# Moving the forget gate's sums one pair of projections back, with their room and their loads in another order

## The chip, the core and the metric

The kernel runs on one core of a Trainium2 chip. The metric is the time of one execution on the device in microseconds (us), the median of several runs; lower is better. TensorE (PE in the rows) multiplies matrices, VectorE (DVE) and ScalarE (ACT) work on elements, GpSimd (POOL) masks, sets constants and issues some DMAs, and the queue of SyncE (SP) issues nearly all loads.

## What is computed

Two layers of a decoder trunk, float32, 528 tokens (16 learned ones and 512 given) of 1024 channels. Each layer is a half-step feed-forward block, a mixer, and another half-step feed-forward block. The change lies in the mixer of the first layer, the attention, whose reference is, cut to what matters:

```python
def attn_mixer(h, w_in, b_f, w_out):
    proj = h @ w_in                      # 24 strips of 128 columns, and 8 columns of forget gates
    qa, ka, va = heads(0), heads(1), heads(2)      # 8 stick-breaking heads of 64
    qb, kb, vb = heads(3), heads(4), heads(5)      # 8 forgetting heads of 64
    log_f = jax.nn.log_sigmoid(f_logit + b_f)
    c = jnp.cumsum(log_f, axis=1)                  # the forget gate's sums, 8 heads x 528 tokens
    ...
    s = jnp.einsum('bhqd,bhkd->bhqk', qb, kb) * scale
    s = s + c[:, :, q0:q1, None] - c[:, :, None, :q1]
    p = jax.nn.softmax(jnp.where(causal, s, -jnp.inf), axis=-1)
    ...
    return jnp.concatenate([o_sb, o_fox], axis=-1) @ w_out
```

The sums `c` are added to the scores of the forgetting heads. They are needed at the first scores of those heads, and no sooner.

## The kernel before

Every product is made at float32 accuracy out of three products of rounded parts: high by high, high by low, low by high. So each weight tile is split, a high part written by ScalarE (`w_hi`) and a low part by VectorE (`w_lo`), and TensorE reads both.

The projections (24 strips) are four plain strips and then ten pairs of strips, `ph.pairs[0]` to `ph.pairs[9]`; pair n holds the strips `p.f` = 4 + 2n and the next. With `QK = 16`, pair 6 (`p.f == QK`) is the first of the pairs that give values; the pairs before it give queries and keys. A pair is computed with seven quarter-size products instead of eight (`qkv_pe`): TensorE's order in pair n is product 1 of n, product 3 of n-1, product 2 of n, product 6 of n, product 4 of n-1, product 7 of n, product 5 of n, each of 12 matmuls. Each has weights of its own. VectorE makes their low parts in a fixed order written out in `attn_dve`: `s23_low` (L2240, for product 6), then drains and sums of weights (L1352, L2213, L1345, L2219, L2224), `s14_low` (L2245, for product 5), for the query and key pairs a low part of the results (L1319), `a_low` of the next pair (L2229, for its products 1 and 2), more drains (L1338, L1359, L1365), and `a22_low` of the next pair (L2234, for its product 4). ScalarE goes through a matching order of its own (`attn_act`).

The forget gate's chain lies between these steps. ScalarE has its logarithm ready long before. At the end of pair 6, VectorE ends the gate (L1436) and sums it over the tokens (L1438, the scan); this counts `fg_step` up to 5. In pair 7 ScalarE writes the high parts of the sums, with both signs (L1195, L1196, `c_high`), and at the end of pair 7 VectorE the low parts (L1441, L1442, `c_low`). GpSimd then stores the four rows of parts to memory (`c_dram`, L3294, `c_stored`).

The gate, its logarithm, the sums and a row of ones (`fg`, `fg_abs`, `fg_sum`, `fg_one`) are the slots 0 to 3 of `fg_room`. That room is shared: the slots are where the first head's queries `sb_qq`, `sb_ql` (slots 0 and 1), its forgetting queries `fx_qq` (slot 2) and its forgetting keys `fx_kk` (slot 3) are loaded later.

`stage_heads` writes out the order of SyncE's queue: the keys of the first head (4 loads), after the wait for `c_low` the queries and the forgetting queries and keys (8 loads), after the wait for `c_stored` two rows twice of the sums (`stage_sums`, 4.1 KB each), then four weight strips of the output projection (`fetch_out`, 512 KB each). The first two strips go as soon as `a22_low` of pair 8 is done, the other two once `a22_low` of pair 9 is. All 14 loads of the first head count one semaphore, `staged[0]`. TensorE waits for all of them at `first_scores`, in pair 9 between its products 4 and 7.

## Time and profile before

| what | us |
|---|---|
| median of 3 runs | 1757.29 (1756.66 to 1757.46) |
| the profiled execution, its time | 1756.96 |
| its span on the core | 1755.2 |
| TensorE busy | 1739.5 |
| VectorE busy | 1401.1 |
| ScalarE busy | 939.0 |
| GpSimd busy | 71.8 |

The span is what the engines' records cover; the time also has what lies around it, 1.76 us here. Busy time is summed from each engine's records, with matmul ends modelled. In a timeline row, a number in brackets is time in which the engine stood idle ahead of the instruction, with what ended it; a matmul's record lasts 0.28 us while the next one starts 0.12 us after it, so the distance between starts tells more of TensorE than the records' lengths.

### The profile page before, as it was taken

To read this page: it belongs to the slowest core of one execution; us is meant where nothing else is said; L and a number is where in the kernel's file an instruction comes from. 1 tells how busy PE (TensorE), PEld (TensorE's weight loads), DVE (VectorE), ACT (ScalarE), POOL (GpSimd) and SP (SyncE) were. 2 spreads that over 40 slices of the span, in tenths; PEclk is the share of its full clock that TensorE was granted. 3 is DMA by queue.
4 is the path that set the end of the run, shared out by engine and by line. 5 is a ranking of instruction groups with operands and counts; after the bars stand their busy time and mean duration, and the time that the engine had idled before them with its cause. 6 is when DMAs were issued, how large, how long until landed. Compare 5 with 4: busy or idle time off the path is not lost.

```text
span 1755.2 us, 34355 instructions
## 1 busy us (share of the span) xinstructions
PE 1739.5 (99%) x13600; PEld 1693.1 (96%) x13600; DVE 1401.1 (80%) x2018; ACT 939.0 (53%) x1554; POOL 71.8 (4%) x193
## 2 busy tenths in 40 slices
PE   8999999999999999999999999999999999999998
PEld 8999999999998899999999999999999988899997
DVE  6856998789988858848998688489987788499875
ACT  6433655555578844625655546246555445266555
POOL 0000000002122202000000000000000000000000
PEclk9999999999999999999999999999999999999999
DMA  5243333236655332333343323333342323343332
GB/s 159 85 121 97 97 108 110 80 103 197 196 157 149 88 109 85 97 97 97 97 119 92 102 87 108 97 96 97 97 113 74 91 77 104 89 114 110 97 95 74
DMA packets 334087, 187.01 MB, mean 107 GB/s; under 512 B 17713, under 2 KB 324593, under 8 KB 333937
## 3 DMA queue, kind: packets, MB, share of 16 engines
q1 hardware_dynamic: 330144, 175.31, 35.6%
q0 software_dynamic: 2960, 8.98, 1.4%
q8 instruction: 106, 1.74, 0.4%
q10 hardware_dynamic: 832, 0.62, 0.1%
q14 instruction: 45, 0.36, 0.1%
HBM read 171.58 MB, written 10.88 MB: 104 GB/s over the span
## 4 chain that ended last, share of the span: by engine, by line
PE 88%; DVE 8%; issue 2%; ACT 1%; DMA 1%; POOL 0%; DVEq 0%; ACTq 0%; SPq 0%; POOLq 0%
PE pair L2820 50%; PE pair L2792 18%; PE pair L2761 8%; PE pair L3156 4%; PE pair L2807 1%; PE pair L968 1%; PE pair L988 1%; PE pair L3032 1%; PE pair L2998 1%; DVE sums_w L2213 1%; DVE w_lo L2245 1%; DVE w_lo L2240 1%; DVE qk_lo L1319 1%; PE pair L903 0%; PE pair L885 0%
## 5 line engine op out<-in xcount | busy, mean ns | idle before, releaser
L2820 PE MATMUL pair<-b_hi,w_hi 128*128 128x264 f32 (+1 forms) x1464 | 415.9, 284 | 0.0
L2820 PE MATMUL pair<-b_lo,w_hi 128*128 128x264 f32 (+1 forms) x1464 | 415.0, 283 | 0.0
L2820 PE MATMUL pair<-b_hi,w_lo 128*128 128x264 f32 (+1 forms) x1464 | 414.6, 283 | 0.0
L2820 PEld LDWEIGHTS pair<-b_hi,w_hi 128*128 128x128 f32 x1464 | 275.7, 188 | 0.9 <-issue 0.5
L2820 PEld LDWEIGHTS pair<-b_hi,w_lo 128*128 128x128 f32 x1464 | 275.7, 188 | 0.0
L2820 PEld LDWEIGHTS pair<-b_lo,w_hi 128*128 128x128 f32 x1464 | 275.6, 188 | 0.0
L1738 ACT ACTIVATE w_hi<-sums_w 128x1024 fp32r<-128x1024 f32 x188 | 198.6, 1057 | 104.7 <-PE pair L2820 60.9
L1738 ACT ACTIVATE w_hi<-raw_all 128x1024 fp32r<-128x1024 f32 (+1 forms) x188 | 158.9, 845 | 141.9 <-PE pair L2820 101.2
L2820 PE MATMUL pair<-blocks_hi,w_hi 128*128 128x264 f32 (+1 forms) x816 | 231.3, 283 | 0.3 <-ACT parts L1925 0.3
L2820 PE MATMUL pair<-blocks_lo,w_hi 128*128 128x264 f32 (+1 forms) x816 | 231.5, 284 | 0.0
L2820 PE MATMUL pair<-blocks_hi,w_lo 128*128 128x264 f32 (+1 forms) x816 | 230.8, 283 | 0.0
L2792 PE MATMUL pair<-b_hi,w_lo 128*128 128x264 f32 (+1 forms) x766 | 173.8, 298 | 0.0
L2792 PE MATMUL pair<-b_hi,w_hi 128*128 128x264 f32 (+1 forms) x766 | 173.5, 298 | 0.0
L2792 PE MATMUL pair<-b_lo,w_hi 128*128 128x264 f32 (+1 forms) x766 | 173.4, 298 | 0.0
L2131 DVE TENSOR_TENSOR w_lo<-raw_all,w_hi 128x1024 fp32r<-128x1024 f32 x117 | 142.6, 1221 | 28.2 <-ACT w_hi L1709 28.2
L1709 ACT ACTIVATE w_hi<-raw_all 128x1024 fp32r<-128x1024 f32 x117 | 121.7, 1050 | 63.3 <-PE pair L2792 58.8
L2820 PEld LDWEIGHTS pair<-blocks_hi,w_hi 128*128 128x128 f32 x816 | 153.8, 188 | 0.7 <-ACT parts L1925 0.5
L2820 PEld LDWEIGHTS pair<-blocks_hi,w_lo 128*128 128x128 f32 x816 | 153.7, 188 | 0.0
L2820 PEld LDWEIGHTS pair<-blocks_lo,w_hi 128*128 128x128 f32 x816 | 153.5, 188 | 0.2
L2240 DVE TENSOR_TENSOR w_lo<-sums_w,w_hi 128x1024 fp32r<-128x1024 f32 x94 | 114.8, 1221 | 24.0 <-ACT w_hi L1738 24.0
L2637 DVE SCALAR_TENSOR_TENSOR h<-pair,h 128x528 f32<-128x528 f32 (+1 forms) x61 | 42.9, 703 | 109.0 <-PE pair L2792 108.4
L2245 DVE TENSOR_TENSOR w_lo<-sums_w,w_hi 128x1024 fp32r<-128x1024 f32 x94 | 114.6, 1219 | 17.8 <-ACT w_hi L1738 17.6
(355 smaller groups left out, 3788.1 us busy)
## 6 DMA issues: line engine op xcount, KB each, us to landing
raw_all<-in_w_ffn_in SPq DMA_DIRECT2D x173, 512.0 KB, 4.0
raw_all<-in_w_ffn_out SPq DMA_DIRECT2D x64, 512.0 KB, 4.4
raw_all<-in_w_ffn_out SPq DMA_DIRECT2D x32, 384.0 KB, 3.7
raw_all<-in_w_attn_in SPq DMA_DIRECT2D x24, 512.0 KB, 4.7
q_all<-qk_dram SPq DMA_DIRECT2D x48, 132.0 KB
qk_dram<-qk_hi POOLq DMA_DIRECT2D x16, 264.0 KB, 4.5
qk_dram<-qk_lo POOLq DMA_DIRECT2D x16, 264.0 KB, 3.0
raw_all<-in_w_attn_out SPq DMA_DIRECT2D x8, 512.0 KB, 4.9
```

What stands on the lines that cost most here:

```text
L968: mm = nc.tensor.matmul(o_main[:, 0, q0 - META:SEQ], head_v[e][:, 0, 3 - s, :], w[:, 0:nq], start=(g == 0), stop=True, skip_group_check=True)
L988: mm = nc.tensor.matmul(own, head_v[e][:, 1, b, :], turned_p[s][:, b, :], start=(g == 0 and b == 0), stop=True, skip_group_check=True)
L1709: nc.scalar.activation(w_hi[j][:, :], raw[j][:, :], ACT.Copy).then_inc(hi_ready, 1)
L1738: return nc.scalar.activation(dst, src, ACT.Copy)
L2131: nc.vector.tensor_tensor(w_lo[j][:, :], raw[j][:, :], w_hi[j][:, :], ALU.subtract).then_inc(lo_ready, 1)
L2240: nc.vector.tensor_tensor(w_lo[1][:, :], S23, w_hi[1][:, :], ALU.subtract).then_inc(s23_lo, 1)
L2245: nc.vector.tensor_tensor(w_lo[2][:, :], s14(p.q), w_hi[2][:, :], ALU.subtract).then_inc(s14_lo, 1)
L2637: nc.vector.scalar_tensor_tensor(hm, pair_of(OUT_BANK[m], ph.last), 0.5, hm, ALU.mult, ALU.add).then_inc(drained, 1)
L2761: mm = nc.tensor.matmul(psum[j][:, bank, c0:c0 + cols], w[j][:, blk], rhs[v][:, k, t0:t0 + cols], start=(k == 0 and w is w_hi and v == 0), ...
L2792: mm = nc.tensor.matmul(bank_of[:, bank, c0:c0 + cols], w[slot][:, blk], rhs[v][:, k, from_:from_ + cols], start=(k == 0 and w is w_hi and ...
L2820: mm = nc.tensor.matmul(dst, w[slot][:, c0 + kk * P:c0 + (kk + 1) * P], rhs(v, kk), start=(fresh and kk == 0 and w is w_hi and v == 0), st ...
L3156: mm = nc.tensor.matmul(psum[j][:, bank, c0:c0 + cols], w[j][:, blk], X[v][:, k, t0:t0 + cols], start=(k == 0 and w is w_hi and v == 0), s ...
```

## The change

The gate's end and the scan move from the end of pair 6 to the end of pair 7 (`p.f == QK + 2`). ScalarE's high parts move from pair 7 to pair 8. VectorE's low parts move from the end of pair 7 into pair 8, behind `s14_low` and ahead of `a_low` of pair 9. Sums and ones change their slots of `fg_room`: the ones now lie where `fx_qq` comes, the sums where `fx_kk` comes. The loads of the queries and of `fx_qq` wait for the scan (`fg_step` at 5), those of `fx_kk` for `c_low`, and the four strips of the output projection come ahead of the loads of the sums. No instruction is added or taken away but for waits.

```diff
--- before.py
+++ after.py
@@ -290,7 +290,7 @@
             turned_p.append(c_room[:, at:at + (i + 2) * P].rearrange("p (b q) -> p b q", q=P).bitcast(F32))
         probs = [qk_room[:, 5 * P:7 * P], b0_rows[:, 1, 7, :], sq, qk_room[:, 0:5 * P]]
 
-        fg, fg_abs, fg_sum, fg_one = (fg_room[0:NH, i, :] for i in range(4))
+        fg, fg_abs, fg_one, fg_sum = (fg_room[0:NH, i, :] for i in range(4))
         fg_both, fg_low = fg_room[:, 0, :], fg_room[LOW_ROW:, 0, :]
         qkv_x = v_rows[:, :, :].rearrange("p (b a) t -> p b (a t)", a=2)
         c_dram = nc.dram_tensor("c_dram", [4, NH, T], F32).ap()
@@ -793,13 +793,17 @@
                 sp.wait_ge(qk_stored[i], stored_before(QK + i))
             sp.wait_ge(aug_ones, 3)
             stage_keys(0, 0)
+            sp.wait_ge(fg_step, 5)
+            stage_queries(0, 0)
+            put(0, fx_qq[0][0:HD, :], part(0, 0, 8))
+            put(0, fx_qq[0][HD:P, :], part(0, 1, 8))
             sp.wait_ge(c_low, 2)
-            stage_queries(0, 0)
-            stage_forgetting(0, 0)
+            put(0, fx_kk[0][0:HD, :], part(0, 0, 12))
+            put(0, fx_kk[0][HD:P, :], part(0, 0, 12))
+            for j in range(4):
+                fetch_out(j)
             sp.wait_ge(c_stored, 16)
             stage_sums(0, 0)
-            for j in range(4):
-                fetch_out(j)
             sp.wait_ge(p5_done, ph.pairs[-1].s + 1)
             stage_queries(0, 1)
             sp.wait_ge(aug_ones, 6)
@@ -1190,7 +1194,7 @@
                 if prev is not None:
                     p1_copy(ph, p, two)
                     s14_high(p, prev)
-                    if prev.f == QK:
+                    if prev.f == QK + 2:
                         act.wait_ge(fg_step, 5)
                         nc.scalar.activation(c_parts[:, 0, :], fg_sum, ACT.Copy).then_inc(c_high, 1)
                         nc.scalar.activation(c_parts[:, 2, :], fg_sum, ACT.Copy, scale=-1.0).then_inc(c_high, 1)
@@ -1417,6 +1421,12 @@
                     s14_low(p)
                     if prev.f < QK:
                         qk_low(prev.f)
+                    if p.f == QK + 4:
+                        dve.wait_ge(c_high, 2)
+                        nc.vector.tensor_tensor(c_parts[:, 1, :], fg_sum, c_parts[:, 0, :],
+                                                ALU.subtract).then_inc(c_low, 1)
+                        nc.vector.tensor_tensor(c_parts[:, 3, :], c_parts[:, 0, :], fg_sum,
+                                                ALU.subtract).then_inc(c_low, 1)
                 if prev is not None and nxt is not None:
                     a_low(nxt)
                 c11_out(p)
@@ -1430,16 +1440,12 @@
                     bottom_scaled(prev)
                 if nxt is not None:
                     a22_low(nxt)
-                if p.f == QK:
+                if p.f == QK + 2:
                     dve.wait_ge(fg_act, 3)
                     dve.wait_ge(fg_step, 3)
                     nc.vector.scalar_tensor_tensor(fg, fg, 0.0, fg_abs, ALU.min, ALU.subtract).then_inc(fg_step, 1)
                     dve.wait_ge(fg_step, 4)
                     nc.vector.tensor_tensor_scan(fg_sum, fg_one, fg, 0.0, ALU.mult, ALU.add).then_inc(fg_step, 1)
-                elif p.f == QK + 2:
-                    dve.wait_ge(c_high, 2)
-                    nc.vector.tensor_tensor(c_parts[:, 1, :], fg_sum, c_parts[:, 0, :], ALU.subtract).then_inc(c_low, 1)
-                    nc.vector.tensor_tensor(c_parts[:, 3, :], c_parts[:, 0, :], fg_sum, ALU.subtract).then_inc(c_low, 1)
 
             def dve_mask(hp, g):
                 s, c = g % 4, STEPS * hp + g
```

On VectorE, around the end of pair 6, before (L1436 and L1438 are the gate's end and the scan, `w_lo<-sums_w` at L2240 is the low part for product 6 of pair 7):

```order
L1365 SCALAR_TENSOR_TENSOR qk_room<-qk_room,qkv_scale,rinv 128x528 [waits drained]
L2234 TENSOR_TENSOR w_lo<-raw_all,w_hi 128x512 [waits hi_ready]
L1436 SCALAR_TENSOR_TENSOR fg_room<-fg_room 8x528 [waits fg_step,fg_act]
L1438 SCALAR_TENSOR_TENSOR fg_room<-fg_room 8x528 [waits fg_step]
L2240 TENSOR_TENSOR w_lo<-sums_w,w_hi 128x1024 [waits s23_hi]
L1319 TENSOR_TENSOR qk_lo<-qk_room,qk_hi 128x528 [waits qk_high_done]
L1352 TENSOR_TENSOR v_rows<-pair,qkv_parts 128x264 [waits qkv_t_lo,u4_out,p7_done]
```

And now (all lines of this part of the program are 4 to 6 higher; L2246 was L2240):

```order
L1369 SCALAR_TENSOR_TENSOR qk_room<-qk_room,qkv_scale,rinv 128x528 [waits drained]
L2240 TENSOR_TENSOR w_lo<-raw_all,w_hi 128x512 [waits hi_ready]
L2246 TENSOR_TENSOR w_lo<-sums_w,w_hi 128x1024 [waits s23_hi]
L1323 TENSOR_TENSOR qk_lo<-qk_room,qk_hi 128x528 [waits qk_high_done]
L1356 TENSOR_TENSOR v_rows<-pair,qkv_parts 128x264 [waits qkv_t_lo,u4_out,p7_done]
```

The two steps of the gate no longer stand ahead of the low part for product 6 of pair 7. On VectorE from the end of pair 7 to `a_low` of pair 9, before:

```order
L1441 TENSOR_TENSOR c_room<-fg_room,c_room 8x528 [waits c_high]
L1442 TENSOR_TENSOR c_room<-c_room,fg_room 8x528
L2240 TENSOR_TENSOR w_lo<-sums_w,w_hi 128x1024 [waits s23_hi]
L1352 TENSOR_TENSOR v_rows<-pair,qkv_parts 128x264 [waits qkv_t_lo,u4_out,p7_done]
L2213 TENSOR_TENSOR sums_w<-raw_all 128x2x512 [waits s23_lo,s14_lo,landed3,landed2]
L1345 SCALAR_TENSOR_TENSOR v_rows<-pair,qkv_scale,rinv 128x264 [waits qkv_t_lo,unit_done]
L2219 TENSOR_TENSOR sums_w<-sums_w,raw_all 128x512 [waits s13_done]
L2224 TENSOR_TENSOR sums_w<-sums_w,raw_all 128x512 [waits s2_done]
L2245 TENSOR_TENSOR w_lo<-sums_w,w_hi 128x1024 [waits s14_hi]
L2229 TENSOR_TENSOR w_lo<-raw_all,w_hi 128x1024 [waits hi_ready]
```

And now:

```order
L1446 SCALAR_TENSOR_TENSOR fg_room<-fg_room 8x528 [waits fg_step,fg_act]
L1448 SCALAR_TENSOR_TENSOR fg_room<-fg_room 8x528 [waits fg_step]
L2246 TENSOR_TENSOR w_lo<-sums_w,w_hi 128x1024 [waits s23_hi]
L1356 TENSOR_TENSOR v_rows<-pair,qkv_parts 128x264 [waits qkv_t_lo,u4_out,p7_done]
L2219 TENSOR_TENSOR sums_w<-raw_all 128x2x512 [waits s23_lo,s14_lo,landed3,landed2]
L1349 SCALAR_TENSOR_TENSOR v_rows<-pair,qkv_scale,rinv 128x264 [waits qkv_t_lo,unit_done]
L2225 TENSOR_TENSOR sums_w<-sums_w,raw_all 128x512 [waits s13_done]
L2230 TENSOR_TENSOR sums_w<-sums_w,raw_all 128x512 [waits s2_done]
L2251 TENSOR_TENSOR w_lo<-sums_w,w_hi 128x1024 [waits s14_hi]
L1426 TENSOR_TENSOR c_room<-fg_room,c_room 8x528 [waits c_high]
L1428 TENSOR_TENSOR c_room<-c_room,fg_room 8x528
L2235 TENSOR_TENSOR w_lo<-raw_all,w_hi 128x1024 [waits hi_ready]
```

The gate's two steps stand where the low parts of the sums stood, and those stand behind L2251 (`s14_low` of pair 8, before L2245) and ahead of `a_low` of pair 9 (L2235, before L2229). On SyncE's queue, the staging of the first head, before:

```order
L747 DMA sb_kk<-qk_dram 64x544 [waits aug_ones,qk_stored1,qk_stored0]
L747 DMA sb_kk<-qk_dram 64x544
L747 DMA fx_qc<-qk_dram 64x528
L747 DMA fx_kc<-qk_dram 64x528
L747 DMA q_all<-qk_dram 64x528 [waits c_low]
L747 DMA q_all<-qk_dram 64x528 x5
L747 DMA fx_kk<-qk_dram 64x528 x2
L747 DMA fx_qc<-c_dram 2x528 [waits c_stored]
L747 DMA fx_kc<-c_dram 2x528
L1621 DMA raw_all<-in_w_attn_out 128x8x128 [waits lo_ready] x4
```

And now:

```order
L747 DMA sb_kk<-qk_dram 64x544 [waits aug_ones,qk_stored1,qk_stored0]
L747 DMA sb_kk<-qk_dram 64x544
L747 DMA fx_qc<-qk_dram 64x528
L747 DMA fx_kc<-qk_dram 64x528
L747 DMA q_all<-qk_dram 64x528 [waits fg_step]
L747 DMA q_all<-qk_dram 64x528 x5
L747 DMA fx_kk<-qk_dram 64x528 [waits c_low]
L747 DMA fx_kk<-qk_dram 64x528
L1627 DMA raw_all<-in_w_attn_out 128x8x128 [waits lo_ready] x4
L747 DMA fx_qc<-c_dram 2x528 [waits c_stored]
L747 DMA fx_kc<-c_dram 2x528
```

The wait for `c_low` moved from the first load of `q_all` to the first of `fx_kk`, and the four loads of 128x8x128 (a strip of 512 KB each) now stand ahead of the two from `c_dram`.

## Rows read from the trace of the kernel before

**Rows 1.** The page's part 1: busy time, share of the span, instructions.

```profile
PE 1739.5 (99%) x13600; PEld 1693.1 (96%) x13600; DVE 1401.1 (80%) x2018; ACT 939.0 (53%) x1554; POOL 71.8 (4%) x193
```

**Rows 2.** Busy time in the stretches of pairs 6, 7, 8: stretch, length, engines, clock.

```profile
457.82:468.04 10.22, 10.22 (x86) 10.22 (x85) 10.02 (x15) 5.83 (x9) 2.16 (x4) 1.00 0.69 210
468.04:479.56 11.52, 10.76 (x87) 10.34 (x85) 11.42 (x17) 6.47 (x10) 1.33 (x4) 1.00 0.60 174
479.56:489.75 10.19, 10.19 (x86) 10.19 (x85) 10.12 (x15) 4.98 (x7) 0.58 (x1) 1.00 0.57 158
```

**Rows 3.** Timeline of TensorE, pair 7: start, length, instruction, idle before.

```profile
473.02 0.51 PE L2820 MATMUL pair<-qkv_t,w_hi 128*128 128x264 f32 x2 [0.44 <-DVE w_lo L2240]
...
477.98 0.53 PE L2820 MATMUL pair<-qkv_t,w_hi 128*128 128x264 f32 x2 [0.32 <-DVE w_lo L2245]
```

**Rows 4.** Timeline of VectorE, end of pair 6 and pair 7.

```profile
469.88 0.69 DVE L1436 SCALAR_TENSOR_TENSOR fg_room<-fg_room 8x528 f32<-8x528 f32 x1
...
471.78 1.19 DVE L2240 TENSOR_TENSOR w_lo<-sums_w,w_hi 128x1024 fp32r<-128x1024 f32 x1
...
476.71 1.22 DVE L2245 TENSOR_TENSOR w_lo<-sums_w,w_hi 128x1024 fp32r<-128x1024 f32 x1
```

**Rows 5.** Timeline of VectorE, end of pair 7 to pair 9.

```profile
481.13 0.69 DVE L1441 TENSOR_TENSOR c_room<-fg_room,c_room 8x528 fp32r<-8x528 f32 x1
...
482.37 1.21 DVE L2240 TENSOR_TENSOR w_lo<-sums_w,w_hi 128x1024 fp32r<-128x1024 f32 x1
...
487.83 1.22 DVE L2229 TENSOR_TENSOR w_lo<-raw_all,w_hi 128x1024 fp32r<-128x1024 f32 x1
...
490.51 0.68 DVE L2234 TENSOR_TENSOR w_lo<-raw_all,w_hi 128x512 fp32r<-128x512 f32 x1
```

**Rows 6.** Timeline of TensorE: the start of pair 9, and its first scores.

```profile
489.75 0.28 PE L2820 MATMUL pair<-b_hi,w_hi 128*128 128x264 f32 x1
...
497.92 0.34 PE L885 MATMUL pair<-q_all,sb_kk 128*128 128x144 f32 x2
```

**Rows 7.** Timeline of SyncE's queue: issues, from `c_low` on.

```profile
482.47 3.97 SPq L747 DMA_DIRECT2D q_all<-qk_dram  x6
486.48 1.24 SPq L747 DMA_DIRECT2D fx_kk<-qk_dram  x2
...
488.24 0.26 SPq L747 DMA_DIRECT2D fx_kc<-c_dram  x1
488.55 1.01 SPq L1621 DMA_DIRECT2D raw_all<-in_w_attn_out  x2
...
491.77 1.60 SPq L1621 DMA_DIRECT2D raw_all<-in_w_attn_out  x1
```

**Rows 8.** DMA issues at 488.55 and at 491.77: KB each, us to landing.

```profile
raw_all<-in_w_attn_out SPq DMA_DIRECT2D x1, 512.0 KB, 5.0
...
raw_all<-in_w_attn_out SPq DMA_DIRECT2D x1, 512.0 KB, 6.9
```

**Rows 9.** Two short stretches; the last columns: clock, DMA share, GB/s.

```profile
497.00:497.25 0.25, 0.25 (x4) 0.25 (x4) 0.00 (x0) 0.06 (x1) 0.00 (x0) 1.00 0.51 143
...
498.00:498.25 0.25, 0.25 (x5) 0.25 (x3) 0.13 (x1) 0.00 (x0) 0.00 (x0) 1.00 0.07 18
```

**Rows 10.** DMA issues at 514.98, and at 3.42 (behind a load of 512 KB).

```profile
head_v<-v_tok SPq DMA_DIRECT2D x1, 4.0 KB, 2.3
...
raw_all<-in_w_ffn_in SPq DMA_DIRECT2D x3, 128.0 KB, 5.6
```

**Rows 11.** GpSimd's store of the sums, its landing, and the slowest store near.

```profile
483.13 0.58 POOL L3294 DMA_DIRECT2D c_dram<-c_room  x1 [8.40 <-DVE c_room L1442]
...
DMA to landing us min/median/max: 3.2/3.2/3.2
...
qk_dram<-qk_lo POOLq DMA_DIRECT2D x1, 264.0 KB, 7.0
```

**Rows 12.** A stretch near the program's start, columns as in rows 2.

```profile
6.00:8.00 2.00, 0.06 (x1) 0.00 (x0) 1.28 (x3) 1.25 (x4) 0.00 (x0) 1.00 1.08 344
```

## The prediction

> **What bounds the kernel now.** I read the page's busy times first. TensorE is busy for 99% of the span [rows 1], so an edit in VectorE's order can only win back waits of TensorE. The second view is the busy time pair by pair. Pair 6 takes 10.22 us and pair 8 takes 10.19, but pair 7 takes 11.52, in which VectorE is busy for 11.42 [rows 2]. Here alone VectorE sets the pace. The third view, TensorE's timeline, shows where: it waits in pair 7 for the low part of product 6 and again for that of product 5 [rows 3]. Together the two cost 11.52 - 10.22 = **1.30 us**. The idle figures (0.44 and 0.32) are smaller than that, since a matmul's record hides the first 0.16 us of a gap and the first matmuls after a wait take about 0.11 us more; that is 0.27 us a wait. The fourth view, VectorE's timeline, gives the cause: the gate's end and the scan stand from 469.88 to 471.78, 1.90 us, right ahead of the low part that TensorE waits for [rows 4].
>
> **Where TensorE would want what.** Seven equal products in 10.22 us are 1.46 us each. Product 6 of a pair begins 3 x 1.46 = 4.38 us after the pair's start, product 5 begins 6 x 1.46 = 8.76 after it. Without waits, pair 7 (start 468.04) wants its low parts at 472.42 and 476.80, pair 8 would start at 479.56 - 1.30 = 478.26 and want them at 482.64 and 487.02, and pair 9 would start at 488.48, when it wants `a_low`.
>
> **The steps on VectorE.**
> (a) Out of the end of pair 6: -1.90 us on VectorE. The low part for product 6 of pair 7 then starts at 469.88 and takes 1.19: done at 471.07, wanted at 472.42. The one for product 5 was done at 476.71 + 1.22 = 477.93 [rows 4], now at 476.03, wanted at 476.80. Both waits go: **-1.30 us**. ScalarE's high parts and the drains' inputs are there in time (TensorE is at the same place as before until 472.42).
> (b) End of pair 7: the two low parts of the sums, 482.37 - 481.13 = 1.24 us [rows 5], go, and the 1.90 us of gate and scan come. The low part for product 6 of pair 8 started at 482.37; now at 482.37 - 1.90 - 1.24 + 1.90 = 481.13, done at 482.34, wanted at 482.64. It fits by 0.30: nothing.
> (c) `s14_low` of pair 8 is as much earlier, 1.24 us: it ends 487.83 + 0.07 - 1.24 = 486.7, wanted at 487.02. It fits by 0.3 us.
> (d) The 1.24 us of low parts now stand ahead of `a_low` of pair 9, whose start comes out at exactly the old 487.83 [rows 5], since what was moved sums to zero by then. It ends at 489.05, and TensorE, now 1.30 us earlier, wants it at 488.48. With 0.05 us to notice it starts at 489.10: a new wait of 0.62 plus 0.11 for the start after it, **+0.73 us**. Pair 9 started at 489.75 before [rows 6], so 0.65 us would be left by its start and 0.65 - 0.11 = 0.54 after the slower first matmuls, to set against 1.30 - 0.73 = 0.57. I take 0.55.
> (e) ScalarE's two high parts stand in pair 8 instead of pair 7; it is busy for 4.98 of 10.19 us there [rows 2], so they cost nothing.
> So up to the first scores the sum is **-0.55 us**: TensorE reaches them at 497.92 - 0.55 = 497.37 [rows 6].
>
> **The steps on SyncE's queue.** There TensorE waits for all 14 loads of the first head. Before, the wait was met long ahead: the last load of the sums was issued at 488.24 [rows 7].
> (f) Queries and `fx_qq` now wait for the scan, which ends near 481.1, a little before the old 482.47. Nothing.
> (g) `c_low` comes at 487.90 instead of 482.44. The two loads of `fx_kk` are issued then and take 1.28 us as before (486.48 to 487.76, of which 1.24 are issues) [rows 7], so the first strip of the output projection goes at 489.2 instead of 488.55: 0.66 us later.
> (h) Strips 3 and 4 wait for `a22_low` of pair 9, which is where it was (490.51 + 0.68) [rows 5]. Strip 4 was issued at 491.77 and its issue lasted 1.60 us, where the two first ones took 1.01 together [rows 7]; I read that as a full queue. So SyncE is free for the sums at 493.4, or at 494.0 if the queue drains 0.66 us later. Their store is done by then: issued about 0.7 us after `c_low`, landed 3.2 us later [rows 11], 491.8. The two loads of the sums go at 494.0 and 494.5 at the latest.
> (i) Now the landing, of which the trace has no row for this load. Below: a load of 4 KB with nothing big ahead landed in 2.3 us [rows 10], which gives 496.8 and no wait. Above: it lands with strip 4, which was issued at 491.77 and landed 6.9 us later, at 498.67 [rows 8], now 0.66 later, 499.33. Between: at 497.1 half of the 16 engines had run dry, and a few packets went on to 498.2 [rows 9]. If the sums lie on one of the queues that are done early, they land at 497.1 + 0.66 + 0.5 = 498.3; the 0.5 is what lay between strip 4's last packet and its landing. I put the loads behind the strips, since loads of 128 KB behind one of 512 KB took 5.6 us [rows 10] and since the strips themselves landed later and later (5.0, then 6.9 us) [rows 8]. The middle of 498.3 and 499.3 is 498.8. TensorE starts there at 498.8 + 0.05, with 0.11 for the start: 498.96 against 497.92, so **+1.0 us** net (bounds of this case +0.5 and +1.6).
> The Trainium skill ("DMA: Bandwidth & Descriptors", section "Why a DMA increments its semaphore by 16 and not by 1") has a rule that speaks for the early end: a copy is split over as many of the 16 engines as divide its slowest dimension, so two rows would wait for the strips' share on two engines alone, not for strip 4's landing. No row of this trace shows on which engines the sums lie. By that page the time would be 1757.8, by the landing of strip 4 it would be 1758.9.
> (j) After the scores, VectorE and ScalarE wait for TensorE's first scores anyway, so what TensorE loses shifts everything behind it and is not caught up. A pause of 1.5 us or so leaves the clock alone as far as rows go: TensorE stood for nearly 2 us near the start and the granted clock stayed at 1.00 [rows 12].
>
> **Sum.** -1.30 + 0.73 + about 1.6 at the first scores = +1.0 us. On the profiled execution's 1756.96 (span 1755.2 and 1.76 around it) that is 1758.0. The median of the runs is 0.33 higher, 1757.29, and gives **1758.3**.
>
> **The rivals.**
> Rival 1, the sums are not held up by the strips: the wait for `staged[0]` is met in time, as before. For it: 4 KB in 2.3 us, issued at 494.0 to 494.5, is there at 496.8, ahead of 497.37. Against it: the landings as read above [rows 8, 10]. Then only -0.55 is left: 1756.7. If the order on VectorE also leaves no wait at `a_low`, -1.3: 1756.0.
> Rival 2, slower, the store of the sums: it comes when the strips are on their way instead of before them. It took 3.2 us; a store to memory that met two loads of 512 KB took 7.0 us [rows 11]. With 7.0 it lands at 495.6, the loads go at 495.6 and 496.1 and land at 498.4 at the earliest, more likely at 499 to 500 behind the strips: +1.2 to +2.2, so 1759.2 in the middle. It turns into over 0.2% (3.5 us) only if the sums land after 501.3, that is if the store takes some 9 to 10 us, more than any row near here.
> Rival 3, the change does not do what it says: the waits of pair 7 stay. VectorE's time of 11.42 in 11.52 us speaks against it, and (a) leaves 0.8 and 1.4 us of room. Then all costs come without the gain: 1759.6.
>
> **How the numbers follow.** The forecast (+0.5 to +1.6) gets 0.58, rival 1 gets 0.24, rival 2 gets 0.12 (0.02 of it over 0.2%), rival 3 gets 0.02, and 0.04 is left for what I don't see, half of it slower by over 0.2%. A measurement of this kernel can tell about 0.2%, 3.5 us, from no change; none of the cases reaches that but the far end of rival 2. So faster 0.01, same 0.95, slower 0.04. The range takes in rival 1 without its far end and rival 2's middle: 1756.4 to 1759.6.
>
> **What would show it.** Right: pair 7 at about 10.2 us without a wait of TensorE; one wait of TensorE at the start of pair 9 for the low part of `raw_all` (`a_low`), near 0.45 us as idle figures go; a wait of about 1.3 us at the first product of `q_all` and `sb_kk`, released by a DMA. The prediction is wrong if that last wait is absent (rival 1), or if the loads of the sums are issued later than 494.5 because of the store (rival 2), or if TensorE waits in pair 8, where my room is 0.3 us twice.

## The result and the profile after

| what | before | changed |
|---|---|---|
| median of 18 executions | 1757.37 us (1756.34 to 1758.02) | 1760.11 us (1758.78 to 1761.92) |
| the profiled execution, its time | 1756.96 | 1760.04 |
| its span | 1755.2 | 1758.3 |
| TensorE busy | 1739.5 | 1741.6 |

The ratio is 1.0018, with a 95% interval of 1.0012 to 1.0025. The changed kernel is 2.7 us slower. I had forecast 1758.3 and a range up to 1759.6, so the sign was right and the time lies outside the range. The ratio lies within the 0.2% that I had named as the bound of "the same"; its interval reaches past it.

The page's first part shows more busy time of TensorE with the same number of instructions. Waits don't count as busy, so matmuls themselves got slower somewhere:

```profile
PE 1741.6 (99%) x13600; PEld 1695.1 (96%) x13600; DVE 1401.1 (80%) x2018; ACT 939.2 (53%) x1554; POOL 72.0 (4%) x193
```

The two longest waits of TensorE from 380 to 525 us (what it waited for: us in total, times, longest):

```profile
PE pair L889 <- DMA fx_kc<-c_dram: 1.8, 1, 1.8
PE pair L2826 <- DVE w_lo L2235: 0.4, 1, 0.4
```

The two waits of pair 7 [rows 3] are gone and the two predicted ones have come: at `a_low` of pair 9 (L2235) and at the first scores (L889). The pairs' stretches, pair 7 and then pair 8 with the new wait behind it, answer to [rows 2]:

```profile
468.18:478.40 10.22, 10.22 (x87) 10.22 (x86) 10.12 (x16) 5.54 (x8) 1.33 (x4) 1.00 0.60 182
478.40:489.20 10.80, 10.37 (x86) 10.16 (x84) 10.73 (x15) 6.19 (x10) 0.49 (x1) 1.00 0.45 127
```

Pair 7 lasts 10.22 us instead of 11.52, and pair 8 lasts 10.80 with the wait instead of 10.19. Now TensorE's timeline from pair 9 on (start, length, instruction, idle before), which answers to [rows 6]:

```profile
489.20 0.39 PE L2826 MATMUL pair<-b_hi,w_hi 128*128 128x264 f32 x1 [0.43 <-DVE w_lo L2235]
...
497.34 0.28 PE L2826 MATMUL pair<-qkv_t,w_lo 128*128 128x264 f32 x1
...
499.44 0.42 PE L889 MATMUL pair<-q_all,sb_kk 128*128 128x144 f32 x2 [1.81 <-DMA fx_kc<-c_dram]
...
500.92 1.34 PE L876 MATMUL pair<-ident,v_rows 128*128 128x128 f32 x8
...
502.72 0.64 PE L2826 MATMUL pair<-qkv_t,w_hi 128*128 128x264 f32 x2
...
505.17 0.40 PE L2826 MATMUL pair<-qkv_t,w_hi 128*128 128x264 f32 x2
...
506.26 1.03 PE L876 MATMUL pair<-ident,v_rows 128*16 128x128 f32 x8
```

And the same transposes in the kernel before, on either side of the same product 7:

```profile
499.32 1.04 PE L872 MATMUL pair<-ident,v_rows 128*128 128x128 f32 x8
...
503.11 1.03 PE L872 MATMUL pair<-ident,v_rows 128*16 128x128 f32 x8
```

From one set of transposes to the next it was 3.79 us and is now 5.34. No wait lies between them: two matmuls of one shape last 0.64 us at 502.72 and 0.40 us at 505.17. The stretches of 1 us around them tell why (columns as in [rows 2]; the last three numbers are the granted clock, the DMA share and GB/s):

```profile
501.00:502.00 1.00, 1.00 (x10) 1.00 (x8) 0.82 (x5) 0.94 (x4) 0.00 (x0) 0.76 0.00 0
502.00:503.00 1.00, 1.00 (x7) 1.00 (x6) 0.70 (x2) 1.00 (x6) 0.52 (x3) 0.50 0.00 0
...
504.00:505.00 1.00, 1.00 (x7) 1.00 (x6) 0.93 (x6) 0.47 (x2) 0.52 (x1) 0.54 0.00 0
505.00:506.00 1.00, 1.00 (x10) 1.00 (x9) 0.23 (x1) 0.00 (x0) 0.00 (x0) 1.00 0.14 33
```

The clock column reads 0.50, the lower of the two levels (1.2 GHz instead of 2.4), for 3.4 us (from 501.5 to 504.9) behind the pause of 1.81 us, and TensorE gets through 6 or 7 matmuls in 1 us instead of 10 or 11.

The account between the two traces, at TensorE: the start of the program +0.14 (pair 7 begins at 468.18 instead of 468.04); pair 7, pair 8 and the wait at pair 9 together -0.60 (the scores could start at 497.34 + 0.12 = 497.46, 29.28 us after pair 7's start instead of 29.88); the wait for the sums 499.44 - 497.46 = +1.98; the scores, 1.48 us instead of 1.40, +0.08; half the clock, 5.34 - 3.79 = +1.55. Together that is +3.15, and the spans differ by 3.1. What lies behind 506 us is only shifted.

SyncE's queue shows where the wait for the sums is from (start and length of the issues; answers to [rows 7]):

```profile
489.19 5.26 SPq L1627 DMA_DIRECT2D raw_all<-in_w_attn_out  x4
...
491.32 1.55 SPq L1627 DMA_DIRECT2D raw_all<-in_w_attn_out  x1
492.92 1.53 SPq L1627 DMA_DIRECT2D raw_all<-in_w_attn_out  x1
494.50 1.03 SPq L747 DMA_DIRECT2D fx_qc<-c_dram  x1
495.57 0.26 SPq L747 DMA_DIRECT2D fx_kc<-c_dram  x1
```

The first row is the group of four strips, the next two are strips 3 and 4 of it by themselves. Each of these two now blocks the queue for over 1.5 us (before, only the last one did), and the first load of the sums, of 4.1 KB, takes 1.03 us to issue. The second is out at 495.8.

### The profile page after: what moved, and what is told of

The parts are those of the page before. It is cut to its first block, busy times and chain, and to the rows that moved or that the text cites. A ratio compares the mean times of both kernels' runs of the same rounds, so it can differ in the third digit from the quotient of the medians.

```text
span 1758.3 us, 34355 instructions
## 1 busy us (share of the span) xinstructions
PE 1741.6 (99%) x13600; PEld 1695.1 (96%) x13600; DVE 1401.1 (80%) x2018; ACT 939.2 (53%) x1554; POOL 72.0 (4%) x193
## 4 chain that ended last, share of the span: by engine, by line
PE 86%; DVE 9%; issue 2%; DMA 1%; ACT 1%; SPq 0%; DVEq 0%; POOL 0%; ACTq 0%; POOLq 0%
PE pair L2826 49%; PE pair L2798 18%; PE pair L2767 8%; PE pair L3162 4%; PE pair L2813 1%; PE pair L972 1%; PE pair L992 1%; PE pair L3004 1%; DVE sums_w L2219 1%; DVE w_lo L2251 1%; PE pair L3038 1%; DVE w_lo L2246 1%; DVE qk_lo L1323 1%; PE pair L907 0%; PE pair L889 0%
## 5 line engine op out<-in xcount | busy, mean ns | idle before, releaser
L2246 DVE TENSOR_TENSOR w_lo<-sums_w,w_hi 128x1024 fp32r<-128x1024 f32 x94 | 114.8, 1221 | 24.1 <-ACT w_hi L1744 24.1
L2251 DVE TENSOR_TENSOR w_lo<-sums_w,w_hi 128x1024 fp32r<-128x1024 f32 x94 | 114.6, 1219 | 17.6 <-ACT w_hi L1744 17.6
```

What stands on the lines that cost most here:

```text
L2246: nc.vector.tensor_tensor(w_lo[1][:, :], S23, w_hi[1][:, :], ALU.subtract).then_inc(s23_lo, 1)
L2251: nc.vector.tensor_tensor(w_lo[2][:, :], s14(p.q), w_hi[2][:, :], ALU.subtract).then_inc(s14_lo, 1)
```

## The experiments

The theory that the runs are to test has two parts. First, all of the loss hangs on one thing, the sums' loads behind four strips on one queue. Second, the wait costs twice: its own length, and then a lower clock that the pause brings on. The rival to the first part was that the low parts ahead of `a_low` or the new room are what costs; the rival to the second was that the lower clock has another cause than the pause. The runs were made in three groups, each against the kernel before on the same chip: 1757.11 us in the first and in the second group (33 executions each), 1757.20 in the third (26). The program begins at slightly different times in the traces: pair 7 starts at 468.18 in the changed kernel's, and between 467.37 and 468.72 in the others. Where times of two traces are set against each other, they are therefore counted from the start of pair 7.

**The sums ahead of the strips.** The changed kernel with one edit:

```diff
-            for j in range(4):
-                fetch_out(j)
             sp.wait_ge(c_stored, 16)
             stage_sums(0, 0)
+            for j in range(4):
+                fetch_out(j)
```

> The changed kernel, but on SyncE's queue the two loads of the sums come ahead of the four strips again. Theory: of the changed kernel's 2.7 us, 1.5 are TensorE's longer way to the first scores, because the loads of the sums stand behind 2 MB of strips, and 1.6 are matmuls at half rate right after that pause. Then here the sums land near 495.5 (store issued 488.7, landed 3.5 us later, load 2.5 us), TensorE does not wait at the first scores, its clock does not fall, and only the -0.55 us of the new order on VectorE is left: 0.9997 of the kernel before, 1756.8 us. Rival, the late store of the sums is at fault, not the strips: then the wait at the first scores stays, 1 us or more, and the time is 1758.5 or above.

Measured 1756.97, ratio 0.9998 (0.9989 to 1.0007). SyncE's issues, and TensorE at the first scores:

```profile
491.18 0.26 SPq L747 DMA_DIRECT2D fx_qc<-c_dram  x1
...
491.79 5.23 SPq L1627 DMA_DIRECT2D raw_all<-in_w_attn_out  x4
```

```profile
496.95 0.34 PE L889 MATMUL pair<-q_all,sb_kk 128*128 128x144 f32 x2
```

No wait, no lower clock, and the whole loss is gone. SyncE waits 2.6 us for the store (488.6 to 491.18) with the strips behind it, and that costs nothing either. So without the new order of these issues the rest of the change has no loss.

**The kernel before, with the strips ahead of the sums and nothing else.**

```diff
             stage_forgetting(0, 0)
+            for j in range(4):
+                fetch_out(j)
             sp.wait_ge(c_stored, 16)
             stage_sums(0, 0)
-            for j in range(4):
-                fetch_out(j)
```

> The kernel before, with one edit: the four strips come ahead of the loads of the sums on SyncE's queue. VectorE's order, the room and the waits are those of before. Theory: strip 4 is issued at 491.8 and lands at 498.7 as before, the sums are issued at 493.4 and land with it; TensorE wants them at 497.92 and waits some 0.8 to 1.0 us: +0.9 us, 1758.3, if the clock holds through so short a pause, +2.5, 1759.9, if it falls as in the changed kernel (there the pause was 1.97 us). Rival, loads overtake the strips: no wait, 1757.4.

Measured 1756.78, ratio 0.9998 (0.9989 to 1.0007): no loss. Here my expectation missed. The issues, strip 4's landing (KB, us) and the first scores:

```profile
487.11 4.50 SPq L1621 DMA_DIRECT2D raw_all<-in_w_attn_out  x4
...
491.03 0.58 SPq L1621 DMA_DIRECT2D raw_all<-in_w_attn_out  x1
491.65 1.07 SPq L747 DMA_DIRECT2D fx_qc<-c_dram  x1
492.77 0.26 SPq L747 DMA_DIRECT2D fx_kc<-c_dram  x1
```

```profile
raw_all<-in_w_attn_out SPq DMA_DIRECT2D x1, 512.0 KB, 7.3
```

```profile
497.31 0.34 PE L885 MATMUL pair<-q_all,sb_kk 128*128 128x144 f32 x2
```

The first strips leave at 487.11 and are partly gone by the time of strip 4, whose issue takes 0.58 us instead of 1.53. So the sums are out at 493.0, which is 25.5 us after the start of pair 7 (467.53 here), instead of 27.7. Strip 4 lands at 491.03 + 7.3 = 498.3, yet the scores start at 497.31 without waiting: the loads of the sums had landed before a strip that stood ahead of them in the queue. In the changed kernel it was the same, strip 4 at 492.92 + 7.1 = 500.0 and the scores at 499.44. So the order alone doesn't cost; it costs together with the later `c_low`. That moves the first strip from 19.6 to 21.0 us after pair 7's start, so closer to TensorE's need, and the issues of strips 3 and 4 then block. Neither part does it alone.

**The changed kernel, the pause filled.** At the first scores TensorE gets 14 more matmuls that nobody reads, into a bank that is free there. They add work and leave the computation as it is:

```diff
+                wait_v_copy(pe, 0)
+                for i in range(14):
+                    nc.tensor.matmul(psum[3][:, 0, 0:HALF], w_hi[3][:, 0:P], qkv_t[0][:, T4, 0:HALF],
+                                     start=True, stop=True, skip_group_check=True)
```

> The changed kernel with 14 more matmuls of TensorE (128x264, their result is never read) right ahead of the first scores, 14 x 0.12 = 1.7 us, inside the pause of 1.97 us in which it waits for the loads of the sums. Theory: the matmuls at half rate after the pause come from the pause; with work in it the clock stays, the wait's end stays at 499.4, and the time is that of the changed kernel less 1.6: 1758.5 us, ratio 1.0007 to the kernel before. Rival, something else slows TensorE there (its memory ports, the loads): as the changed kernel, 1760.1.

Measured 1759.14, ratio 1.0012 (1.0002 to 1.0021). TensorE's timeline, and the stretch from 502 to 503 us:

```profile
499.67 0.42 PE L889 MATMUL pair<-q_all,sb_kk 128*128 128x144 f32 x2
...
501.15 1.04 PE L876 MATMUL pair<-ident,v_rows 128*128 128x128 f32 x8
...
504.93 1.03 PE L876 MATMUL pair<-ident,v_rows 128*16 128x128 f32 x8
...
531.52 0.45 PE L889 MATMUL pair<-q_all,sb_kk 128*128 128x144 f32 x2 [0.63 <-DMA fx_kk<-qk_dram]
```

```profile
502.00:503.00 1.00, 1.00 (x11) 1.00 (x10) 0.94 (x3) 0.97 (x5) 0.52 (x3) 1.00 0.00 0
```

The scores start as late as in the changed kernel (31.30 and 31.26 us after pair 7's start), but from transposes to transposes it is 3.78 us again, and the clock column reads 1.00. The time came out 0.6 above what I expected, which is the size of the wait at 531.52 (0.63 us) for loads of the next heads. It stands in this trace and in that of the other long filling below, and in no other; why filling causes it is open.

**The sums ahead, and the low parts behind `a_low`.** The first edit, and besides:

```diff
-                    if p.f == QK + 4:
-                        dve.wait_ge(c_high, 2)
-                        ...
                 if prev is not None and nxt is not None:
                     a_low(nxt)
+                if p.f == QK + 4:
+                    dve.wait_ge(c_high, 2)
+                    ...
```

> As a_sums_first, and besides the low parts of the sums stand behind a_low of pair 9 on VectorE instead of ahead of it. Theory: a_low of pair 9 is done at 487.9 instead of 489.1, before TensorE wants it at 488.4, so the third wait (0.43 us idle, 0.7 in time) goes too and all 1.3 us of pair 7 stay won. The low parts of the sums are done at 489.1, their store lands at 493, their loads at 495.7, first scores at 496.7: no wait. 1756.0 us, ratio 0.9993. Rival: the sums land after 496.7 and TensorE waits at the scores for what is missing: as a_sums_first or up to 1 us more.

Measured 1755.90, ratio 0.9993 (0.9984 to 1.0002). The same kernel in the second group:

> d_behind_a_low once more, to narrow its interval. Theory: all three waits of TensorE on VectorE's low parts are gone and none has come at the scores, 1.3 us less than the kernel before: ratio 0.9993. Rival: the 1.2 us measured the first time were within the spread of the runs, ratio 1.0000.

It gave 1756.08, ratio 0.9994 (0.9985 to 1.0003). The first scores in the trace of the first group:

```profile
496.80 0.34 PE L889 MATMUL pair<-q_all,sb_kk 128*128 128x144 f32 x2
```

Pair 7 starts at 468.19 there, so TensorE reaches the scores after 28.61 us, where the kernel before took 29.88: 1.27 us less. No wait for a low part is left among its waits from 460 to 540 us. This is the full gain of the gate's move, 1.0 to 1.2 us in the medians of both groups and about what was expected (1.3 by the trace). Each interval still reaches past 1, so of a faster kernel I can only say that two measurements point the same way.

**The changed kernel again, and with 6 matmuls in the pause.** The second group had the changed kernel once more, and one with 6 of the added matmuls instead of 14:

```diff
-                for i in range(14):
+                for i in range(6):
```

> The changed kernel once more, unchanged, beside the kernels of this group. Theory: as in its own measurement, ratio 1.0018 to the kernel before (about 1760.2 us), with a wait of 1.8 us (idle figure) at the first scores and matmuls 0.22 us apart, instead of 0.12, for about 3 us right after them. Rival, those slow matmuls were one execution's accident: then they are absent here and the time is 1758.6.

> As c_filled, but with 6 matmuls ahead of the first scores instead of 14, 0.73 us of work: the pause that is left before the loads of the sums land is 1.2 us instead of 0.3. Theory, the length of the pause decides: 1.2 us is too short for the clock to fall and the time is that of c_filled, 1759.1, ratio 1.0012. Rival, any wait there of about a microsecond lets the clock fall: 1760.2, ratio 1.0018, and the matmuls after the scores are 0.22 us apart.

The changed kernel gave 1759.87, ratio 1.0015 (1.0006 to 1.0024); the other gave 1758.73, ratio 1.0011 (1.0002 to 1.002). TensorE in the changed kernel's new trace:

```profile
499.61 0.42 PE L889 MATMUL pair<-q_all,sb_kk 128*128 128x144 f32 x2 [1.53 <-DMA fx_kc<-c_dram]
...
501.09 1.04 PE L876 MATMUL pair<-ident,v_rows 128*128 128x128 f32 x8
...
504.88 1.03 PE L876 MATMUL pair<-ident,v_rows 128*16 128x128 f32 x8
```

The pause was 1.53 us in this execution, and the clock stayed: 3.79 us between the transposes, and a time of 1758.85, near my forecast. So one kernel does both. Over all its executions this can be counted by the mean granted clock, which is given to three digits: it is 0.998 or lower in 11 of the first 18 executions and in 4 of the 11 of this group, and never in the 92 executions of the kernel before. The kernel with 6 matmuls still paused 1.56 us in its trace, where I had expected 1.2, since the scores came later in it (31.7 us after pair 7's start instead of 31.3); 2 of its 11 executions are at 0.998. So it tells little.

**The sums issued by ScalarE's queue.** The changed kernel without the two loads in SyncE's queue; ScalarE issues them once they are stored:

```diff
-            sp.wait_ge(c_stored, 16)
-            stage_sums(0, 0)
...
+                        act.wait_ge(c_stored, 16)
+                        for dst, k in ((fx_qc[0][HD:HD + 2, :], 0), (fx_kc[0][HD + 2:HD + 4, :], 2)):
+                            act.dma_start(dst.bitcast(F32), c_dram[k:k + 2, bass.ds(0, 1), :].rearrange(
+                                "k a t -> (k a) t")).then_inc(staged[0], 16)
```

> The changed kernel, but the two loads of the sums are issued by ScalarE, on its own DMA queue, at the place in pair 9 right before its table load; SyncE's queue keeps the strips where the change put them. Theory, the order within SyncE's queue holds the sums back (SyncE comes to them at 494.5 and 495.6, and they stand behind the strips): ScalarE issues them near 493.5, they pass the strips, land at 496 to 497, and TensorE waits little or not at all: 1756.8 to 1757.2, ratio 0.9998. Rival, the 16 engines are busy with the strips whichever queue the sums come by: they land near 499 again and the time is 1759 to 1760.

Measured 1756.27, ratio 0.9998 (0.9989 to 1.0007). Issues of ScalarE's queue, and TensorE:

```profile
491.68 0.24 ACTq L1205 DMA_DIRECT2D fx_qc<-c_dram  x1
491.95 0.28 ACTq L1205 DMA_DIRECT2D fx_kc<-c_dram  x1
```

```profile
497.41 0.41 PE L887 MATMUL pair<-q_all,sb_kk 128*128 128x144 f32 x2 [0.64 <-DMA fx_kc<-c_dram]
```

Pair 7 starts at 467.37 in this trace. Counted from there the two loads are issued 2.0 and 2.8 us sooner than in the changed kernel, with the first strip in the same place (21.0 us), and the scores start 1.2 us sooner (30.0 instead of 31.3). Behind a pause of 0.64 us the clock stayed. A wait of 0.64 us is left: a load of 4 KB took some 5.4 us here (491.95 to 497.4), with three strips issued ahead of it and the fourth at its issue (491.14 to 492.85), where 2.3 us is what it takes with nothing big ahead [rows 10].

**Two strips, the sums, two strips.**

```diff
-            for j in range(4):
+            for j in range(2):
                 fetch_out(j)
             sp.wait_ge(c_stored, 16)
             stage_sums(0, 0)
+            for j in range(2, 4):
+                fetch_out(j)
```

> The changed kernel, but only two of the four strips stand ahead of the loads of the sums, the other two behind. SyncE then comes to the sums when their store has landed, near 492.3. Theory, strips 3 and 4 are what holds the sums back, since SyncE can issue them only from 491.3 on and is busy with strip 4 until 494.5: here the loads land by 496.5, no wait of TensorE, 1756.8 us, ratio 0.9998, and the strips start as early as in the changed kernel. Rival, any strip ahead holds them: the loads land with strip 2 or later and some wait of TensorE is left, 1757.5 or above.

Measured 1756.63, ratio 0.9998 (0.9989 to 1.0007). The first load of the sums, behind two strips:

```profile
491.99 0.26 SPq L747 DMA_DIRECT2D fx_qc<-c_dram  x1
```

```profile
497.17 0.34 PE L891 MATMUL pair<-q_all,sb_kk 128*128 128x144 f32 x2
```

Both are issued in 0.26 us (the second at 492.28) and nobody waits for them. At this place of the program two strips ahead are free and four are not.

**A longer pause, bare and filled.** Two kernels of the third group hold the sums' loads back until TensorE has done the product ahead of the scores, so that the pause grows and depends less on the queue; the second has 20 of the added matmuls in it:

```diff
             sp.wait_ge(c_stored, 16)
+            sp.wait_ge(unit_done, ph.pairs[-2].n + 2)
             stage_sums(0, 0)
```

> The changed kernel with one more wait on SyncE's queue: the loads of the sums are issued only when TensorE has done the product right ahead of the first scores. Their way, 2.3 us at least, then is all pause of TensorE: about 2.8 us, where the changed kernel has 1.5 to 2.0. Theory, a pause of this length lets TensorE's clock fall to half, the longer the pause the surer: here in nearly every execution, the matmuls after the scores are 0.22 us apart for about 3 us, and the time is 1756.8 (the order without a pause) + 2.9 + 1.6 = 1761.3 us, ratio 1.0024. Rival, the half rate in one trace was an accident of that execution: 1759.7, ratio 1.0015.

> As i_long_pause, but with 20 matmuls (2.4 us, their result is never read) in the pause. The loads come as late as there. Theory, it is the idleness of TensorE that costs the clock: no matmul after the scores at half rate, 1.6 us less than i_long_pause: 1759.7, ratio 1.0015. Rival, TensorE is slow there for another reason: as i_long_pause.

The bare one gave 1761.71, ratio 1.0025 (1.0016 to 1.0035), and the filled one 1760.35, ratio 1.0020 (1.0011 to 1.0029). TensorE with the bare pause, and the stretch behind it:

```profile
499.77 0.56 PE L890 MATMUL pair<-q_all,sb_kk 128*128 128x144 f32 x2 [2.04 <-DMA fx_kc<-c_dram]
...
502.41 1.91 PE L877 MATMUL pair<-ident,v_rows 128*128 128x128 f32 x8
```

```profile
500.00:506.00 6.00, 6.00 (x29) 6.00 (x29) 2.81 (x12) 4.33 (x15) 0.82 (x4) 0.50 0.00 0
...
506.00:507.00 1.00, 1.00 (x8) 1.00 (x6) 0.93 (x6) 0.28 (x1) 0.52 (x1) 0.64 0.00 0
```

And with the filled one:

```profile
499.78 0.34 PE L890 MATMUL pair<-q_all,sb_kk 128*128 128x144 f32 x2
...
531.71 0.45 PE L890 MATMUL pair<-q_all,sb_kk 128*128 128x144 f32 x2 [0.95 <-DMA fx_kk<-qk_dram]
```

```profile
501.00:504.00 3.00, 3.00 (x27) 3.00 (x26) 2.79 (x13) 2.90 (x13) 0.84 (x5) 1.00 0.00 0
```

The scores start at nearly the same time in both (31.6 and 31.8 us after pair 7's start). The bare pause was 2.04 us and not the 2.8 that I had expected: the second load was issued at 498.11, so it had landed at most 1.7 us later, and not after the 2.3 of [rows 10]. Behind the bare pause the clock is at 0.50 for 6.8 us, from 499.9 to 506.7 (29 matmuls in the 6 us shown), and behind the filled one at full speed (27 in 3 us). From the scores to the second transposes (508.20) it took 8.43 us in this trace, where the kernel before took 5.19 (497.92 to 503.11): the lower clock cost 3.2 us. This execution has the lowest mean clock of its kernel, and its 1762.47 lies above the median. The mean clock is 0.998 or lower in 8 of 10 executions of the bare one and in none of 11 of the filled one. The medians differ by 1.36 us, and by more without the 0.95 us that the filled one loses at 531.71.

What follows. All kernels in which the sums arrive in time or nearly so run like the kernel before or a little faster, and none of their 66 executions has the lower mean clock. It appears in the kernels whose traces have a bare pause of 1.5 to 2.0 us, in a part of the executions: 25 of 50 in all. With the pause filled it appears in none of 22. These counts are firmer than the times: filling took the ratio from 1.0018 to 1.0012, and the two intervals overlap. That the pause brings it on is shown; what decides within one kernel whether it comes is not. The traces fit a dependence on the pause's length (yes at 2.04 and 1.81 us, no at 1.56, 1.53 and 0.64), but that is five executions.

One remainder stays open. In the changed kernel the 7 executions with a higher mean clock than 0.998 have a mean time of 1759.8, and the other 11 of 1760.6. The first number is still 0.9 above the 1758.9 that the trace's wait alone would give (1757.3 and 1.6). The mean clock is a coarse measure. A fall of 3.4 us takes 0.001 off it, and the end of the span takes off 0.0005 to 0.0013: there the column reads 0.50 after TensorE's last matmul, for 1.7 us in the kernel before and for 4.6 us in the kernel with two strips ahead, whose traces read 1.000 and 0.999 without any fall behind the scores. So an execution with a fall can still read 0.999, and the counts above are lower bounds; by this measure alone a single fall in a filled kernel isn't excluded either. Such hidden falls, or longer waits than in the traces, could fill the 0.9 us; no run separates the two.

## Why the prediction was wrong

**VectorE and pairs 7 to 9, steps (a) to (e): right.** The timeline of VectorE after, against [rows 4, 5]:

```profile
469.99 1.22 DVE L2246 TENSOR_TENSOR w_lo<-sums_w,w_hi 128x1024 fp32r<-128x1024 f32 x1
...
481.26 1.19 DVE L2246 TENSOR_TENSOR w_lo<-sums_w,w_hi 128x1024 fp32r<-128x1024 f32 x1
...
487.94 1.21 DVE L2235 TENSOR_TENSOR w_lo<-raw_all,w_hi 128x1024 fp32r<-128x1024 f32 x1
```

I had 469.88, 481.13 and 487.83, and the whole program begins some 0.12 us later in this trace. Pair 7 takes 10.22 us without a wait (a). Pair 8 has none, so the room of 0.3 us held twice (b, c). The wait at `a_low` is there with 0.43 us of idle time (I had said near 0.45), and it lengthens pair 8 and the wait by 0.61 against [rows 2], where I had 0.62 and 0.11 for the start (d). Up to the scores the gain is 0.60 us, predicted 0.55.

**SyncE's queue, steps (f) and (g): right.** The queries went at 481.36 (the first of six issues), `c_low` came at 488.01 and the first strip at 489.19; I had 481.1, 487.90 and 489.2.

**Step (h), too low by 1.1 us at the last load.** I took the 1.60 us that strip 4 needed to issue [rows 7] as a full queue, and then added only the 0.66 us by which everything is later. In fact strip 3 blocks as well (1.55 us), and the load behind strip 4 does too (1.03 us). So the sums went at 494.50 and 495.57, where I had 494.0 and 494.5 at the latest. A queue that blocks once in the trace of before, where 1.7 us lie between the first two strips and the others, blocked for strip 3, for strip 4 and for the first load of the sums here, where 0.7 us do. That it is full then stays my reading, since no trace shows how full it is. The store was not the cause: issued at 488.71 and landed 3.5 us later, at 492.2, well before the queue came to it. Rival 2 fell by that.

**Step (i), the landing: the size was inside the bounds, by luck.** I had +1.0 at the scores with bounds of +0.5 and +1.6, and it came out at 497.92 to 499.44, +1.52, of which 0.14 is the later start of the program. This would have given 1758.9 for the median, and the traced execution of this kernel without the lower clock took 1758.85. But my upper bound was the landing of strip 4, and the load had passed strip 4 (499.4 against 500.0, and 497.3 against 498.3 in the kernel before with the strips ahead). The reading that a small load lands behind the whole of what is ahead of it was wrong; two errors, a later issue and an earlier landing, offset each other. The Trainium skill ("DMA: Bandwidth & Descriptors", section "Why a DMA increments its semaphore by 16 and not by 1") has a load of two rows wait for two engines' share alone; the two traces agree with that, though none shows the two engines.

**Step (j), the clock: the step that failed.** I said that a pause of 1.5 us leaves the clock alone, since TensorE stood for nearly 2 us near the start and the granted clock stayed at 1.00 [rows 12]. That column can't be read so. Here is TensorE in the kernel before right behind that stretch, and the clock column over it:

```profile
9.60 0.64 PE L3156 MATMUL pair<-b_lo,w_hi 128*128 128x264 f32 x2
...
12.94 0.40 PE L3156 MATMUL pair<-b_lo,w_hi 128*128 128x264 f32 x2
```

```profile
8.00:12.00 4.00, 3.76 (x17) 3.76 (x18) 2.01 (x5) 2.91 (x7) 0.00 (x0) 1.00 1.15 317
```

Two matmuls take 0.64 us at 9.60 and 0.40 us at 12.94, the same two figures as inside and behind the half-speed stretch of the changed kernel. TensorE was at half its rate there while the column read 1.00. The trace explains it: its first clock record begins at 12.7 us, where the matmuls get faster, and ahead of a first record the column reads 1.00 with nothing behind it. So my one piece of evidence that a pause of 2 us is harmless came from an engine that was at half rate already. The row says nothing for the step. I had given the lower clock no term, no rival and no room in the range; it was 1.55 us in the trace. What speaks for it having carried the median past 1759.6 is the kernel with the pause filled: its ratio of 1.0012 on 1757.37 would be 1759.5, inside the range, and it has a wait of 0.63 us in it that the changed kernel has not. It is no proof, since 4 of the 7 executions without a lower mean clock are above 1759.6 too.

**The rivals.** The pattern of rival 1 (the sums are not held up) is what the kernels with the sums ahead or behind two strips do: 1756.97 and 1756.63 against its 1756.7. Its further end, without the wait at `a_low`, is the kernel with the low parts behind it: 1755.90 and 1756.08 against 1756.0. Rival 3 (pair 7's waits stay) didn't come.

## What to carry to other kernels

A small load that another engine waits for goes ahead of the big ones, or on a queue of its own: four loads of 512 KB ahead of it cost 2 us of waiting here, two of them nothing, and four of them nothing where they left 1.4 us sooner. An issue that took over 1 us in the trace of before is a warning that others may block as well once they stand closer together. A new pause of TensorE like this one may cost its length a second time in slower matmuls behind it, so give that a term or a rival of its own. Test the clock by the distance between matmuls of one shape and not by the clock column alone.

## What the runs showed of the hardware

Behind a bare pause of 1.81 and of 2.04 us TensorE ran at half rate for 3.4 and for 6.8 us. By the mean clock this came in at least 23 of the 39 executions of these two kernels, the changed one (whose pause was 1.53 us in another trace, with no fall) and the one with the longer pause, and in none of the 22 with 14 or 20 matmuls in the pause. It began at once in one trace (at 499.9, with the scores at 499.77) and some 2 us after the restart in the other (at 501.5, with the scores at 499.44).

The issue of a 512 KB load on SyncE's queue took 0.50 us as the third of four in the kernel before and 1.55 us in the changed kernel, and as the fourth 1.60 and 1.53 us, but 0.58 in the kernel before with the strips ahead of the sums. Behind four of them even a load of 4.1 KB took 1.03 and 1.07 us to issue. A load of two rows then landed before a load of 512 KB that was ahead of it in the same queue (499.4 against 500.0, and by 497.3 against 498.3).
